# Third and fourth weight sum of a feed-forward pair: from VectorE to accumulating transfers issued by GpSimd

## What is computed

```python
def swiglu(h, w_in, w_out):
    gate, up = jnp.split(h @ w_in, 2, axis=-1)
    return (jax.nn.silu(gate) * up) @ w_out

x = x + FFN_HALF * swiglu(rmsnorm(x, ffn1_norm[l]), ffn1_w_in[l], ffn1_w_out[l])
```

## Time and profile before

| | |
|---|---|
| median of 3 runs | 2616.46 us (2616.0 to 2618.01) |
| profiled execution, its own time | 2617.89 us |
| its span, first to last instruction | 2616.1 us |
| PE busy | 2595.7 us (99%) |
| DVE busy | 2030.0 us (78%) |
| ACT busy | 1543.6 us (59%) |
| GpSimd busy | 116.4 us (4%) |
| read from HBM | 466.09 MB |

### The profile page before, as it was taken

One profiled execution on the slowest core, in us unless ns is written; L12 is line 12 of the kernel. 1 busy time (PEld: TensorE's weight loads), 2 busy tenths in 40 slices (PEclk: granted clock), 3 DMA queues, 4 the chain that ended last, 5 costly groups with the idle time before them and its releaser, 6 DMA issues.

```text
span 2616.1 us, 34886 instructions
## 1 busy us (share of the span) xinstructions
PE 2595.7 (99%) x14187; PEld 2212.1 (85%) x14187; DVE 2030.0 (78%) x2073; ACT 1543.6 (59%) x1701; POOL 116.4 (4%) x146
## 2 busy tenths in 40 slices
PE   9999999999999999999999999999999999999998
PEld 7889998888888899888888889978888889978887
DVE  8887854699799686557998995676997995677887
ACT  6656674465565567644656555555656555655655
POOL 0000170000000003400000000000000000000000
PEclk9999999999999999999999999999999999999999
DMA  6746545466465555545757465444755646544663
GB/s 217 239 160 195 158 142 191 139 219 232 146 233 176 170 163 163 178 133 181 237 166 233 164 205 176 156 145 153 241 194 186 208 162 191 158 143 142 215 230 105
DMA packets 353822, 473.99 MB, mean 181 GB/s; under 512 B 28727, under 2 KB 278911, under 8 KB 353408
## 3 DMA queue, kind: packets, MB, share of 16 engines
q1 hardware_dynamic: 349246, 469.86, 55.0%
q10 hardware_dynamic: 4418, 1.90, 0.3%
HBM read 466.09 MB, written 5.64 MB: 180 GB/s over the span
## 4 chain that ended last, share of the span: by engine, by line
PE 88%; DVE 5%; ACT 3%; POOLq 2%; issue 1%; DVEq 1%; DMA 0%; SPq 0%; ACTq 0%; POOL 0%
PE bank L421 27%; PE bank L423 26%; PE bank L422 26%; PE bank L974 1%; DVE w_lo L408 1%; POOLq L2460 1%; POOLq L2463 1%; ACT w_hi L402 1%; PE bank L558 1%; DVE conv_acc L2223 1%; PE bank L1841 1%; DVE neg_max L2773 0%; PE bank L2716 0%; ACT scores L2734 0%; DVE scores L2766 0%
## 5 line engine op out<-in xcount | busy, mean ns | idle before, releaser
L421 PE MATMUL bank<-w_hi,xn_hi 128*128 128x512 f32 (+2 forms) x1856 | 705.6, 380 | 1.7 <-DVE xn_lo L538 1.4
L423 PE MATMUL bank<-w_hi,xn_lo 128*128 128x512 f32 (+2 forms) x1856 | 692.4, 373 | 0.0
L422 PE MATMUL bank<-w_lo,xn_hi 128*128 128x512 f32 (+2 forms) x1856 | 691.5, 373 | 0.0
L408 DVE TENSOR_TENSOR w_lo<-raw,w_hi 128x2048 fp32r<-128x2048 f32 (+2 forms) x190 | 412.1, 2171 | 219.1 <-ACT w_hi L402 218.6
L402 ACT ACTIVATE w_hi<-raw 128x2048 fp32r<-128x2048 f32 (+3 forms) x199 | 359.7, 1809 | 151.3 <-PE bank L423 147.0
L1094 ACT ACTIVATE w_hi<-raw 128x2048 fp32r<-128x2048 f32 x192 | 367.3, 1913 | 136.0 <-DMA raw<-in_ffn_w_out 40.7
L1202 DVE TENSOR_TENSOR w_lo<-raw,w_hi 128x2048 fp32r<-128x2048 f32 x192 | 438.0, 2281 | 1.7 <-ACT w_hi L1094 1.6
L421 PEld LDWEIGHTS bank<-w_hi,xn_hi 128*128 128x128 f32 x1856 | 350.1, 189 | 65.8 <-issue 5.9
L423 PEld LDWEIGHTS bank<-w_hi,xn_lo 128*128 128x128 f32 x1856 | 349.7, 188 | 61.8
L422 PEld LDWEIGHTS bank<-w_lo,xn_hi 128*128 128x128 f32 x1856 | 350.4, 189 | 56.5
L421 PE MATMUL bank<-w_hi,hid_hi 128*128 128x512 f32 x704 | 278.2, 395 | 0.0
(11 more groups left out here) (397 smaller groups left out, 3917.7 us busy)
## 6 DMA issues: line engine op xcount, KB each, us to landing
raw<-in_w_in SPq DMA_DIRECT2D x122, 1024.0 KB, 5.2
raw<-in_ffn_w_in SPq DMA_DIRECT2D x126, 512.0 KB, 5.2
raw<-in_ffn_w_out SPq DMA_DIRECT2D x44, 1024.0 KB, 5.2
raw<-in_ffn_w_down SPq DMA_DIRECT2D x44, 1024.0 KB, 5.2
raw<-in_ffn_w_gate SPq DMA_DIRECT2D x64, 512.0 KB, 4.3
raw<-in_ffn_w_up SPq DMA_DIRECT2D x64, 512.0 KB, 5.5
block<-in_ffn_w_in SPq DMA_DIRECT2D x48, 512.0 KB, 7.1
block<-in_ffn_w_gate SPq DMA_DIRECT2D x24, 512.0 KB, 6.4
```

Source lines behind the costliest of these rows:

```text
L408: dve.tensor_tensor(in_order(kind, slot, w_lo), as_loaded(kind, slot), in_order(kind, slot, w_hi).bitcast(F32), ALU.subtract).then_inc(s_l ...
L421: pe.matmul(out, a_hi, b_hi, start=start, stop=False, skip_group_check=check)
L422: pe.matmul(out, a_hi, b_lo, start=False, stop=False, skip_group_check=check)
L423: return pe.matmul(out, a_lo, b_hi, start=False, stop=stop, skip_group_check=check)
```

## The change

DVE keeps the sums `t1` and `t2`. The other two are made by transfers that add what they bring to what stands in their target: GpSimd issues, for each pair, two transfers of 512 KB that add block 22 of the weights to `b12` once `t1` is formed (the third sum), and two that add block 21 to `t2` once the low half of `t2` is made (the fourth sum, now in `t2` instead of `t14`). A transfer can only add here, so the signs of the sums of weights and of x are changed such that all four weight sums are plain sums, and some outputs are subtracted instead of added. ACT's high halves of `t3` and `t4` wait for the new transfers. The raw slot of `b21` no longer has to outlive the fourth sum. The weights of `b21` and `b22` are read from HBM twice.

```diff
@@ Phase.raw_freed
         i = self.former(j, raw_slots)
-        if i >= 0 and self.items[i][0] == "b21":
-            u = self.items[i][1]
-            i = self.items.index(("t3" if u == TWOS[0] else "b22", u))
         return self.base + (i + 1 + START)
...
+        s_third = sem("third_sum_in_b12")
+        s_fourth = sem("fourth_sum_in_t2")
...
-        SUMS = ("t1", "t2", "t3", "t4")
+        SUMS = ("t1", "t2")
...
+        def ffn_pool(pool, p, f, gate_w, gate_at, up_w, up_at):
+
+            def add_block(dst, k, u, done):
+                at = dst[:, :].rearrange("p (k s n) -> p k s n", k=4, s=2)
+                k = slice(4 * k, 4 * k + 4)
+                pool.dma_start(at[:, :, 0, :], cols(gate_w, u * 256 + gate_at)[:, k, :], accum_op=ALU.add).then_inc(done, 16)
+                pool.dma_start(at[:, :, 1, :], cols(up_w, u * 256 + up_at)[:, k, :], accum_op=ALU.add).then_inc(done, 16)
+
+            for u in TWOS:
+                pool.wait_ge(s_block12, 32 * (len(TWOS) * f + TWOS.index(u) + 1))
+                pool.wait_ge(s_sums, count(SUMS, f, u, "t1"))
+                add_block(b12, 1, u + 1, s_third)
+                pool.wait_ge(s_sums, count(SUMS, f, u, "t2"))
+                pool.wait_ge(s_lo, p.base + (FFN_AT["t2", u] + 1 + START))
+                add_block(t2, 1, u, s_fourth)
...
@@ ffn_act, hi; the same table of sources in ffn_dve, lo
-                    src = {"t1": t14, "t2": t2, "b22": b22, "t3": b12, "t4": t14}[kind]
+                    src = {"t1": t14, "t2": t2, "b22": b22, "t3": b12, "t4": t2}[kind]
                     if kind == "b22":
                         act.wait_ge(s_block22, 32 * (len(TWOS) * f + TWOS.index(u) + 1))
+                    elif kind == "t3":
+                        act.wait_ge(s_third, 32 * (len(TWOS) * f + TWOS.index(u) + 1))
+                    elif kind == "t4":
+                        act.wait_ge(s_fourth, 32 * (len(TWOS) * f + TWOS.index(u) + 1))
                     else:
                         act.wait_ge(s_sums, count(SUMS, f, u, kind))
...
@@ ffn_dve
             def sum_t1(u):
                 j = FFN_AT["b11", u]
                 if u - 3 in TWOS:
-                    low_done("t4", u - 3)
+                    low_done("t1", u - 3)
...
-                dve.tensor_tensor(t14[:, :], b12[:, :], raw[p.raws[j]][:, :], ALU.subtract).then_inc(s_sums, 1)
+                dve.tensor_tensor(t14[:, :], b12[:, :], raw[p.raws[j]][:, :], ALU.add).then_inc(s_sums, 1)
...
                 if u - 3 in TWOS:
-                    low_done("t2", u - 3)
-                dve.tensor_tensor(t2[:, :], b22[:, :], t14[:, :], ALU.subtract).then_inc(s_sums, 1)
-
-            def sum_t3(u):
-                dve.tensor_tensor(b12[:, :], b22[:, :], b12[:, :], ALU.subtract).then_inc(s_sums, 1)
-
-            def sum_t4(u):
-                j = FFN_AT["b21", u]
-                dve.wait_ge(s_sums, count(SUMS, f, u, "t2"))
-                low_done("t1", u)
-                dve.tensor_tensor(t14[:, :], t2[:, :], raw[p.raws[j]][:, :], ALU.subtract).then_inc(s_sums, 1)
+                    low_done("t4", u - 3)
+                dve.tensor_tensor(t2[:, :], b22[:, :], t14[:, :], ALU.add).then_inc(s_sums, 1)
...
             def first_ones():
...
-                mix(0, b4[3], x21, ALU.add)
-                mix(2, b4[0], x21, ALU.subtract)
+                mix(0, b4[3], x21, ALU.subtract)
+                mix(2, x21, b4[0], ALU.subtract)
...
-                mix(1, mixed[0][:, :, :], b4[0], ALU.subtract)
+                mix(1, mixed[0][:, :, :], b4[0], ALU.add)
...
-                mix(3, b4[1], mixed[1][:, :, :], ALU.subtract)
+                mix(3, mixed[1][:, :, :], b4[1], ALU.subtract)
...
                 mixed_lo(1)
-                sum_t3(2)
...
                     lo("b21", u + 1)
-                    sum_t3(u + 1)
                     lo("t1", u + 1)
...
             def two(u):
                 lo("t2", u)
-                sum_t4(u)
                 hide(u, 0, bank[4][:, 256:512], gate_act[:, 0, :])
...
-                dve.tensor_tensor(u2[:, :], bank[4][:, :], p1[:, :], ALU.add).then_inc(s_outs, 1)
+                dve.tensor_tensor(u2[:, :], bank[4][:, :], p1[:, :], ALU.subtract).then_inc(s_outs, 1)
...
@@ block.gpsimd
-            pool.wait_ge(s_rest, 16 * n_rest)
-            for l in range(LAYERS):
-                mixer1_pool(pool, l)
+            for b, l in layers:
+                w, g, v, h, _ = ffn_weights[b, 0](l)
+                ffn_pool(pool, in_layer(plans[b], 0, l), ffn_index(b, l, 0), w, g, v, h)
+                if b == 0:
+                    if l == 0:
+                        pool.wait_ge(s_rest, 16 * n_rest)
+                    mixer1_pool(pool, l)
+                w, g, v, h, _ = ffn_weights[b, 1](l)
+                ffn_pool(pool, in_layer(plans[b], 3, l), ffn_index(b, l, 1), w, g, v, h)
```

More of the change, by code:

```diff
@@ L1329, in two @@
                 dve.wait_ge(s_outs, count(OUTS, f, u, "u2"))
-                dve.tensor_tensor(u2[:, :], bank[5][:, :], u2[:, :], ALU.add).then_inc(s_outs, 1)
+                dve.tensor_tensor(u2[:, :], u2[:, :], bank[5][:, :], ALU.subtract).then_inc(s_outs, 1)
                 lo("g0", u + 2)
                 used("t3", u)
-                dve.tensor_tensor(u3[:, :], bank[4][:, :], p1[:, :], ALU.add).then_inc(s_outs, 1)
+                dve.tensor_tensor(u3[:, :], bank[4][:, :], p1[:, :], ALU.subtract).then_inc(s_outs, 1)
                 dve.wait_ge(s_copied, count(COPIES, f, u, "p5"))
                 dve.wait_ge(s_outs, count(OUTS, f, u, "u3"))
-                dve.tensor_tensor(p5[:, :], p5[:, :], u3[:, :], ALU.add).then_inc(s_outs, 1)
+                dve.tensor_tensor(p5[:, :], u3[:, :], p5[:, :], ALU.subtract).then_inc(s_outs, 1)
                 used("t4", u)
-                dve.tensor_tensor(u3[:, :], u3[:, :], bank[5][:, :], ALU.subtract).then_inc(s_outs, 1)
+                dve.tensor_tensor(u3[:, :], bank[5][:, :], u3[:, :], ALU.subtract).then_inc(s_outs, 1)
                 lo("g1", u + 2)
```

## The result

| | before | after |
|---|---|---|
| median | 2616.51 us (2616.0 to 2618.01, 4 runs) | 2634.64 us (2631.97 to 2639.61, 4 runs) |
| profiled execution, its own time | 2617.89 us | 2639.61 us |
| its span | 2616.1 us | 2637.8 us |

The ratio is 1.0070 [1.0058, 1.0082]: 18 us slower. The direction was forecast (2688, and 0.72 for slower), the size was not: +72 was forecast. The profiled execution of after is the longest of its four, so the spans differ by 21.7 us and not by 18.

What follows compares the result with a forecast made beforehand. PE was taken to bound the kernel, busy 2595.7 of 2616.1 us. All terms were 0 but the fourth sum's transfer, 24 x (11.0 - 8.0) = 72 us, giving 2616.5 + 72, so 2688 us; range 2615 to 2780.

Steps and rivals of the forecast that it cites:

- PE is the bound, DVE's work is worth 0: Removing 48 sum instructions frees 109.5 us of DVE, but PE does not wait there: 0, bounds 0 and -1.2 us.
- Signs 0: Adding instead of subtracting, and 6 swapped operand orders, keep each instruction's shape, engine and place: priced at 0.
- Earlier free slot and third sum 0: Raw slot of `b21` freed sooner, 0; third sum's transfers have 21.0 us of room before ACT reads `b12`, 0.
- 24 x (11.0 - 8.0) = 72 us: Fourth sum by transfer: in each of 24 pairs PE stalls by landing time less room, 72 us in all.
- D: Delay from the low half of `t2` to the fourth sum's landing; taken as 11 us, bounds 5.1 and 14.3.
- The room: Delay the fourth sum can have before PE stalls at `t4`; 6.8 to 8.4 us over 24 pairs, mean 8.0.
- the doubled row: Two block pairs in a row from SP, landed in 10.1 us, taken as nearest to an adding pair's doubled traffic.
- rival (a): Fourth transfer hidden, landing in at most 8.2 us; kernel stays at 2616 us (2615 to 2621); chance 0.25.
- First pairs worse: PE's stall before `t4` should be larger in each feed-forward's first pair, with room 6.8 to 7.7 us, than later.
- Rival (c), the clock: Stalls near 3 us in all pairs also lower PE's clock, 1.4 us each: +34, 2722 us; chance 0.12.
- (d): Far slower transfers, landing in over 14.3 us, GpSimd's issue the bottleneck; at 20 us, 2904 us; chance 0.15.
- (e): Faster by over 5 us, DVE's freed 109.5 us shortening PE's spacing or waits outside the feed-forwards; chance 0.03.

Runs made afterwards that it cites:

- third sum alone: Against the changed kernel, the fourth sum goes back to DVE and only the third comes by adding transfer; 2620.02 us, 1.0012 of before.
- one transfer more: The changed kernel with one more adding transfer of 512 KB, into `t14`, ahead of the fourth sum's two; 2728.29 us, 1.0422 of before.
- fourth sum alone: Against the changed kernel, the third sum goes back to DVE and only the fourth comes by adding transfer; 2662.54 us, 1.0173 of before.
- fourth transfer without adding: The changed kernel, but the fourth sum's two transfers bring block 21 into `t2` without adding it; 2618.18 us, 1.0007 of before.
- 59: Not defined in the text; seemingly the changed kernel, called after in the table; 2634.64 us, 1.0070 of before.
- fourth sum in halves: The changed kernel with four fourth-sum transfers of 256 KB, and ACT and DVE making `t4` in two halves; 2622.33 us, 1.0025 of before.

## Why the prediction was right in direction and wrong in size

- **PE is the bound, DVE's work is worth 0: right.** DVE's busy time fell by 98.7 us (109.5 forecast), and in no run did the time fall below that of before by more than its interval.
- **Signs 0: right** (+0.2 us, run alone).
- **Earlier free slot and third sum 0: right inside the feed-forwards but for one pair.** With the third sum alone no gap stands ahead of `t4`. In after `b21` was late once, and that gave the 3.45 us gap; I had priced the loss of this cover at "some 1.4 us a pair", and it came once, at more. Why it came there, the runs leave open. Not forecast at all were the 1 to 2 us of the mixer's chain: GpSimd's part was looked for in the feed-forwards, where it is idle, and not in what else it does.
- **The failed step is the fourth sum, "24 x (11.0 - 8.0) = 72 us".** Both of its numbers were off, and since it is a small difference of two, that decided the size. D was 9.32 us, not 11. The room was 9.0, not 8.0 (measured with one transfer more, where every pair shows it). With these the same step gives 24 x 0.32 = 7.7 us; pair by pair the gaps are 11.1. The way of the cost, a fourth sum that lands later than the room allows, was right; the size of this term was not.
- **D:** the doubled row, 10.1 us for 2 MB by SP, carried 2 MB through the issue and from HBM, where the pair reads 1 MB, and it shared the engines: from 110 to 120 us they moved 3.74 MB in the kernel before (line below), not the 2 MB of the row alone. What doubles is the time of a piece, 105 ns instead of 50; the 2.0 us from the first instruction to the first packet do not. 2 x 2.8 of moving, as under rival (a), would have been 5.6, and 6.4 were measured. The 2 x 0.5 us for the issue were wrong in kind: GpSimd's second instruction ends at 103.31, while packets already run since 102.7, so the issue lies beside the moving.

```profile
DMA packets 2525, 3.74 MB, mean 374 GB/s; under 512 B 80, under 2 KB 2128, under 8 KB 2524
```

- **The room:** "after that every us of delay reaches the `u2` sum" was wrong. Before, ACT's high half of `t4` ended at 107.68 + 1.92 = 109.60, but DVE began the low half only at 110.55, since `u2`'s first sum held it (lines below, DVE in the kernel before). That 0.95 us was slack that was not counted. The shortest way from ACT's start to PE's was in the rows of before too: 1.92 us of ACT, 2.28 and 0.68 of DVE, 4.88 in sum, where 4.89 were measured. Read backwards from PE by it, those rows give 113.90 - 4.88 - 99.8 = 9.2 us, which is what was measured. In the first pair the room was 8.0 us, where 6.7 to 6.8 were forecast.

```profile
109.95 0.68 DVE L1326 TENSOR_TENSOR sum<-bank,product 128x512 f32<-128x512 f32 x1
110.55 2.28 DVE L1202 TENSOR_TENSOR w_lo<-sum_t_t,w_hi 128x2048 fp32r<-128x2048 f32 x1
```

- **First pairs worse: right.** They carry 9.3 of the 11.1 us.
- **Rival (c), the clock:** the fall of the clock is real, and a fall of 3.4 us costs 1.4 to 1.6 us, close to the 1.4 of the estimate. The estimate was lucky in its source: it took the length of a fall from the start of the program, where matmuls stand 0.43 us apart, but the granted clock of that stretch (12 to 14 us) reads 1.00. The rival needed stalls of nearly 3 us in every pair, and after has one of 3.45 there and one of 2.3 in the mixer. It cost 4.3 us in after, and is what makes the fourth sum alone and the longer fourth so dear. (a) had "D at most 8.2"; D was longer, and was nearly hidden by the larger room. (d) and (e) fell.

By the Trainium skill ("DMA: Bandwidth & Descriptors", Anatomy of one DMA) the estimate for the pair was 4.4 us, or 6.8 with the bytes counted twice. From GpSimd's first instruction to the last packet it was 109.1 - 100.7 = 8.4 us. Its fixed 2.0 us have the size of the 2.0 us to the first packet, but the section puts most of them behind the last byte, as the wait for the confirmed write, and there the trace has 0.4 us to ACT's start; the measurement decides. The moving part took 6.4 us against 4.8 by the doubled bytes. The Trainium skill ("Collectives: The Full Stack", Why ReduceScatter is half of AllGather) says of ReduceScatter, which adds in its transfers, that the add costs no time of its own but needs two source reads, two read descriptors for each piece, and so halves the rate; 105 ns against 50 for each KB agrees with that, here on one core.

## What to carry to other kernels

A sum folded into a transfer takes a wait for a whole transfer in place of a few us of an engine; here that engine was not the bound and nothing was won, and whether it pays where it is, no run here shows. It should be asked for in parts, so that what follows the last byte is short. Where a term is the difference of a latency and a room, work out the room backwards from the bound engine by the shortest way through the instructions between, not forwards from where they stood; they may have stood late for another reason. Ask of an engine that gets new work what its old work feeds, even where the two never meet.

## What the hardware showed

- A transfer that adds took 105 ns of a DMA engine for each 1 KB piece, one that writes some 50, also in packets of 1 KB (49 ns each in SP's queue before); and the pieces of the writing one went as 288 packets, those of the adding one as 1056.
- GpSimd's instruction for 512 pieces took 0.78 us when writing, 1.28 (first) and 1.84 us (second) when adding, 2.40 for a third (one transfer more).
- From GpSimd's first instruction to the first packet: 2.0 us when adding, 1.5 when writing (100.23 to 101.7, fourth transfer without adding).
- GpSimd's chain in the mixer was 1 to 2 us longer in 59 after GpSimd had issued transfers earlier in the execution; its instructions were not slower. In after nearly all of it was one pause, behind the first of them, where the kernel has a drain; this pause grew from 0.12 us to 0.64 with 6 transfers, 1.13 with 12 and 1.62 with 18.
- The granted clock fell to 0.50 for 3.4 or 6.8 us behind gaps ahead of `t4` of 2.5 to 4.0 us, often but not always: 15 of 24 with one transfer more, 6 of 9 with the fourth sum only. In the mixer it fell behind waits of 1.5 us (third sum only) and 1.8 us (fourth sum in halves: 0.59 on the mean from 399 to 403, behind a wait that ended at 398.6).
